# One change to a two-block transformer kernel: gated recurrence unrolled and woven, merge projections in split parts, compression by halves

## What is computed

```python
h = rmsnorm(x, g_pre_mix); z = h @ w_in
kc, vc = compress_blocks(k, pe_k, w1_k, w2_k), compress_blocks(v, ...)   # blocks of 32 tokens, stride 16: 31 of them
hid = silu(einsum('bnlgd,ldh->bngh', blocks, w1)); out = einsum('bngh,hd->bngd', hid, w2)
qk = silu(causal_conv(z[q, k], w, b))                     # 4 taps along the tokens
# gated recurrence (mLSTM), 4 heads of 128; b = cumulative sum of logf, m_t = running maximum
dw  = exp(b_t - b_s + i_s - m_t)
sqk = (q @ k.T) * dh**-0.5 * dw;   num = sqk @ v;   den = sum(sqk)
h_ml = num / max(abs(den), exp(-m_t))
h_ml = h_ml * rsqrt(mean(h_ml**2) + EPS) * g;  y_ml = sigmoid(o) * h_ml
gm = sigmoid(g_merge)                                     # three gates of width 1024
y = gm0 * (y_nsa @ w_proj_nsa) + gm1 * (y_ml @ w_proj_ml) + gm2 * (y_mem @ w_proj_mem)
x = x + rmsnorm(y @ w_out, g_post_mix)
```

## Time and profile before

| | before |
|---|---|
| median of 3 runs | 2626.87 us (2626.28 to 2628.6) |
| the profiled execution | 2629.21 us, its span 2627.4 us |
| mean granted TensorE clock of it | 0.962 |
| TensorE busy | 2470.5 us (94%) |
| VectorE, ScalarE, GpSimd busy | 662.8, 900.3, 961.7 us |
| instructions | 28732 |
| the chain that ended last | TensorE 78%, issue 10%, VectorE 4%, ScalarE 4%, GpSimd 3% |

### The profile page before, as it was taken

The page is one execution under the profiler, slowest core; times in us unless marked ns, Lnnn a source line. Parts: engine busy times, 40 slices in busy tenths (PEclk is TensorE's granted clock), DMA queues, the critical chain, the costliest instruction groups (busy, mean ns, idle before and its releaser), DMA issues.

```text
span 2627.4 us, 28732 instructions
## 1 busy us (share of the span) xinstructions
PE 2470.5 (94%) x10828; PEld 1873.9 (71%) x10828; DVE 662.8 (25%) x1319; ACT 900.3 (34%) x1552; POOL 961.7 (37%) x484
## 2 busy tenths in 40 slices
PE   6999999999889889999989999989899999999997
PEld 5888775766677678877858655477656657788776
DVE  1010312033422220113130566454511112201121
ACT  4332322154424343223221455532332223432232
POOL 3444451622352444444432321044222224344444
PEclk9999999999989999999997999899899998999999
DMA  3233234322121223223421110021113232232232
GB/s 132 96 99 96 82 95 131 109 65 68 51 74 49 80 72 96 96 77 96 140 69 40 49 41 29 1 64 48 40 57 94 83 94 65 72 97 96 79 93 92
DMA packets 74470, 204.04 MB, mean 78 GB/s; under 512 B 7184, under 2 KB 24080, under 8 KB 73872
## 3 DMA queue, kind: packets, MB, share of 16 engines
q1 hardware_dynamic: 71296, 191.92, 23.1%
q10 hardware_dynamic: 3088, 10.97, 1.2%
HBM read 199.71 MB, written 2.10 MB: 77 GB/s over the span
## 4 chain that ended last, share of the span: by engine, by line
PE 78%; issue 10%; DVE 4%; ACT 4%; POOL 3%; DMA 0%; ACTq 0%; POOLq 0%; DVEq 0%
PE bank L635 15%; PE bank L636 15%; PE bank L642 15%; PE bank L848 5%; PE bank L1068 3%; PE bank L1311 3%; POOL parts L490 2%; PE bank L785 2%; PE bank L1373 2%; PE bank L1400 1%; PE bank L1382 1%; PE bank L1288 1%; ACT parts L1603 1%; PE bank L681 1%; PE bank L1327 1%
## 5 line engine op out<-in xcount | busy, mean ns | idle before, releaser
L490 POOL TENSOR_TENSOR parts<-slot,parts 128x1024 fp32r<-128x1024 f32 (+2 forms) x344 | 762.3, 2217 | 1066.2 <-ACT parts L1603 1061.9
L635 PE MATMUL bank<-hhi,parts 128*128 128x512 f32 x1776 | 711.7, 401 | 29.6 <-POOL parts L490 18.2
L636 PE MATMUL bank<-hhi,parts 128*128 128x512 f32 x1776 | 699.8, 394 | 0.0
L1603 ACT ACTIVATE parts<-slot 128x1024 fp32r<-128x1024 f32 (+2 forms) x290 | 280.8, 970 | 842.3 <-PE bank L642 776.4
L642 PE MATMUL bank<-hlo,parts 128*128 128x512 f32 x1776 | 441.2, 390 | 0.1
L635 PEld LDWEIGHTS bank<-hhi,parts 128*128 128x128 f32 x1776 | 338.5, 191 | 124.8 <-POOL parts L490 25.2
L636 PEld LDWEIGHTS bank<-hhi,parts 128*128 128x128 f32 x1776 | 338.9, 191 | 72.7 <-issue 3.8
L642 PEld LDWEIGHTS bank<-hlo,parts 128*128 128x128 f32 x1776 | 333.4, 188 | 71.0 <-issue 1.4
L488 POOL TENSOR_TENSOR parts<-slot,lanes 128x1024 fp32r<-128x1024 f32 x54 | 103.5, 1917 | 469.6 <-PE bank L642 170.9
L2186 DVE TENSOR_TENSOR hid<-silu,bank 128x512 f32 (+1 forms) x66 | 45.4, 688 | 650.5 <-PE bank L642 630.5
L848 PE MATMUL bank<-hhi,parts 128*128 128x512 f32 x416 | 116.5, 415 | 3.0 <-POOL parts L490 3.0
(11 more groups left out here) (362 smaller groups left out, 3176.5 us busy)
## 6 DMA issues: line engine op xcount, KB each, us to landing
slot<-w SPq DMA_DIRECT2D x264, 512.0 KB, 3.5
slot<-w SPq DMA_DIRECT2D x88, 256.0 KB, 2.7
slot<-w SPq DMA_DIRECT2D x48, 448.0 KB, 3.2
hid<-w SPq DMA_DIRECT2D x8, 512.0 KB, 3.4
x<-xT ACTq DMA_DIRECT2D x1, 2048.0 KB, 10.6
hid<-headtab ACTq DMA_DIRECT2D x8, 256.0 KB, 3.9
big<-cmpw ACTq DMA_DIRECT2D x1, 2048.0 KB, 7.8
hid<-w SPq DMA_DIRECT2D x8, 256.0 KB, 2.6
```

The costliest lines, as they stand in the source:

```text
L490: pool.tensor_tensor(low, w, high.bitcast(F32), ALU.subtract).then_inc(splits, 1)
L635: pe.matmul(out, high[:, k, :], mhi[:, k, :], start=(start and k == 0), stop=False)
L636: pe.matmul(out, low[:, k, :], mhi[:, k, :], start=False, stop=False)
L1603: act.activation(parts[nth % 2][:, 0, 0:kt, :], slot[j][:, 0:kt, :], ACT.Copy).then_inc(highs, 1)
```

## The change

- Group product 0 is moved ahead of the gate product, the others one place forward; group product 3 is made with `gate_columns` between its 16th and 17th matmul. `gate_columns` also transposes the least normalisers, to columns.
- Compression alternates the two halves of the array at each of its 32 steps, instead of one half after the other.
- `SPREAD` is gone. A head's maxima are spread by one product (`spread_maxima`) while the head before runs. The least normalisers stay as columns.
- The recurrence is unrolled. The v panels of all heads are made once, in four passes with 512 moving columns (`gated_values`); the q and k panels of the next head are woven between scores and outputs of this one. The sums of the scores are made as columns (matmuls of one column, the scores stationary), as are the sums of squares. Normaliser and norm are joined: since the norm divides by the root of the mean of squares, the division by the normaliser is left out and its square enters the columns as EPS times max(den squared, least squared); one root and one reciprocal of four columns, spread once, stand for two reciprocals, an Abs and a root of 512 columns. Head 3's last two steps lie in the memory attention.
- The merge's branch projections are made from split parts, 24 or 12 fp32r matmuls each. All six panels of a turn are split by ScalarE and GpSimd, in `parts[0]`, `parts[1]` and a third buffer of 4 tiles, `quarter`. The 16 tiles of the branch outputs are split once, ahead of the loop.

The diff, cut (the functions of ScalarE and VectorE have the order of their loops here):

```diff
 
 GATES = dict(outs=1, free7=1, gates=1, acts=5, free2=1, dve=4, stats=2, free3=2, turned=1, free6=1)
-SPREAD = dict(scores=8, free4=4, free5=4)
...
+ML = dict(products=16, splits=16, highs=16, free0=6, free1=6, free4=9, free5=9, free6=1, free7=5, mspreads=4,
+          dve=48, exps=16, convs=8, scores=16, outs=4)
+ML_NORM = dict(sqs=4, stats=4, rcp=4, rinv=4, spreads=4, cats=4)
...
-        negM, emb = big8[:, 0:HEADS, :], big8[:, HEADS:2 * HEADS, :]
+        v_gated, gate_decay = big8[:, 0:TT, :], big8[:, TT:2 * TT, :]
+        quarter = tables_r[:, 0:2 * TT * P].rearrange("p (c k n) -> p c k n", c=2, k=TT)
+        merge_parts = (parts[0], parts[1], parts[0], quarter, parts[1], quarter)
+        memt = memh_r[:, :, :].rearrange("p (a b) m -> p a (b m)", b=2)
+        cat_high = [qs_r[:, 0, :], qs_r[:, 1, :], ks_r[:, 0, :], ks_r[:, 1, :], vs_r[:, :], o_r[:, 0, :], o_r[:, 1, :],
+                    var_r[:, :], *(PT_r[:, k, :] for k in range(TT)), *(memt[:, k, :] for k in range(4))]
+        cat_low = [hid_r[:, k, :] for k in range(16)]
...
+                    for p in range(16):
+                        sp.wait_ge(products, n.at("products", p + 1 - RING))
+                        dst = slot[p % RING][:, :, :]
+                        if 2 <= p < 6:
+                            first_v = panel[8] + 2
+                            src = w8[first_v:first_v + 13:4, :, 2 * (p - 2):2 * (p - 2) + 2, :].rearrange("h p k c -> p h (k c)")
+                            dst = dst.rearrange("p (h k) c -> p h (k c)", h=HEADS)
+                        else:
+                            c = p if p < 2 else p - 4
+                            src = w8[panel[8] + 4 * (c // 3) + (0, 1, 3)[c % 3]]
...
@@ -578,13 +610,19 @@
             for p in range(16):
                 split(p, p % RING, p - 1, load=1 + p // RING)
             n.past(NSA)
-            n.past(SPREAD)
-
-            split_turns(HEADS, ML, range(4), (0, 0))
+            for p in range(16):
+                split(p, p % RING, p - 1, load=1 + p // RING)
+            n.past(ML)
+            n.past(ML_NORM)
             for p in range(HEADS):
                 split(p, p, p - 1)
             n.past(MEM2)
-            split_turns(KD, MERGE, (0, 2, 4))
+            with n.turns(pool, KD, MERGE):
+                for q in range(6):
+                    kt = (8, 8, 8, 4, 8, 4)[q]
+                    high, low = (merge_parts[q][:, c, 0:kt, :] for c in range(2))
+                    pool.wait_ge(highs, n.at("highs", q + 1))
+                    pool.tensor_tensor(low, slot[q][:, 0:kt, :], high.bitcast(F32), ALU.subtract).then_inc(splits, 1)
...
+            def norm_columns_spread(i):
+
+                pe.wait_ge(rinvs, n.at("rinv", i + 1))
+                for t in range(TT):
+                    mm = pe.transpose(bank[3][:, t * P:(t + 1) * P], root_ms[:, t:t + 1].to_broadcast([P, P]), ident)
+                mm.then_inc(spreads, 1)
+
             def norm_of_tiles(events):
...
+            def gate_columns():
+
+                emptied(6, 1)
+                emptied(3, 1)
+                for t in range(TT):
+                    for r in (0, 2):
+                        mm = pe.matmul(bank[3][:, 8 * r + 4 * t:8 * r + 4 * t + 4], rows[0:4, r, t * P:(t + 1) * P],
+                                       ident[0:4, 0:4], start=True, stop=True)
+                mm.then_inc(stats, 1)
+
             pe.wait_ge(tables_loaded, 16)
             pe.wait_ge(params_loaded, 16)
             pe.wait_ge(cmp_loaded, 48)
+            group_product(0)
             pe.wait_ge(h32s, n.at("h32s"))
             emptied(7)
...
-            group_product(1)
+            group_product(2)
 
...
-            group_product(2)
-            emptied(6, 1)
-            emptied(3, 1)
-            for t in range(TT):
-                mm = pe.matmul(bank[3][:, 4 * t:4 * t + 4], rows[0:4, 0, t * P:(t + 1) * P], ident[0:4, 0:4],
-                               start=True, stop=True)
-            mm.then_inc(stats, 1)
+            emptied(1, 1)
+            h_panel(3, bank[1][:, :], between=gate_columns)
             n.past(GATES)
 
 
-            group_product(3)
             emptied(0, 2)
             emptied(1, 2)
             pe.wait_ge(dves, n.at("dve", 1))
             width = (GROUPS + 1) * CMP_N
-            for row, b, done in ((slice(0, 64), 3, stats), (slice(64, P), 6, turned)):
-                emptied(b)
-                for l in range(CMP_L):
+            emptied(3)
+            emptied(6)
+            for l in range(CMP_L):
+                for row, b, done in ((slice(0, 64), 3, stats), (slice(64, P), 6, turned)):
                     mm = pe.matmul(bank[b][:, 0:width].rearrange("p (g b) -> p g b", b=CMP_N), w1c[row, l, :],
                                    kvc[row, :, l:l + CMP_S * (CMP_N - 1) + 1:CMP_S],
                                    start=(l == 0), stop=(l == CMP_L - 1))
-                mm.then_inc(done, 1)
+                    if l == CMP_L - 1:
+                        mm.then_inc(done, 1)
             emptied(3, 1)
             pe.matmul(bank[3][:, 0:GROUPS * CMP_N], w2[:, 0:P], hidk, start=True, stop=True).then_inc(stats, 1)
             emptied(6, 1)
...
-            def normed_sum():
...
+            def gated_values(q):
+
+                high, low = (parts[(2 + q) % 2][:, part, :, :] for part in range(2))
+                pe.wait_ge(splits, n.at("splits", 2 + q + 1))
+                for m in range(24):
+                    t, j = (m // 4, m // 2 % 2) if m < 16 else ((m - 16) // 2, m % 2)
+                    if q == 0 and m < 16 and m % 4 == 0:
+                        emptied(4 + t)
+                    out = bank[4 + t][:, :].rearrange("p (h c) -> p h c", h=HEADS)
+                    mm = pe.matmul(out, (hhi if m < 16 else hlo)[:, 2 * q + j, t * P:(t + 1) * P],
+                                   (low if m < 16 and m % 2 else high)[:, j::2, :],
+                                   start=(q == 0 and m < 16 and m % 4 == 0), stop=(q == 3 and m >= 16 and j == 1))
+                mm.then_inc(products, 1)
...
+            def spread_maxima(i):
...
+                pe.matmul(bank[2][:, :], ident[0:4, i:i + 1].to_broadcast([4, P]), rows[0:4, 1, :], start=True,
+                          stop=True).then_inc(mspreads, 1)
...
+            def gated_out(i, j):
+
+                emptied(4 + j % 2, 1 + 2 * i + j // 2 + 1)
+                if j == 0:
+                    emptied(6, 1)
+                    emptied(7, 1 + i)
+                    emptied(3)
+                    pe.wait_ge(cats, n.at("cats", i))
+                for t in range(j, TT):
+                    pe.matmul(bank[3][:, t:t + 1], PT[:, j, t * P:(t + 1) * P], ones[:, 0:1], start=(j == 0 and t == 0),
+                              stop=(j == TT - 1 and t == TT - 1), skip_group_check=True)
+                mm = pe.matmul(bank[7][:, j * P:T], v_gated[:, j, i * P:(i + 1) * P], PT[:, j, j * P:T],
+                               start=(j == 0), stop=(j == TT - 1))
+                if j == TT - 1:
+                    mm.then_inc(outs, 1)
+
+            def gated_squares(i):
+
+                pe.wait_ge(sqs, n.at("sqs", i + 1))
+                for t in range(TT):
+                    mm = pe.matmul(bank[3][:, 4 + t:5 + t], var[:, t * P:(t + 1) * P], ones[:, 0:1], start=True, stop=True)
+                mm.then_inc(stats, 1)
+
+            pe.wait_ge(dves, n.at("dve"))
+            gated_panel(0, 0, 24)
+            spread_maxima(0)
+            gated_panel(1, 0, 24)
+            for q in range(4):
+                gated_values(q)
+            for i in range(HEADS):
+                o, nq, nk = 3 * i + 2, 3 * i + 3, 3 * i + 4
+                last = i == HEADS - 1
+                gated_panel(o, 0, 24)
+                gated_scores(i, 0)
+                gated_scores(i, 1)
+                if not last:
+                    gated_panel(nq, 0, 4)
+                gated_out(i, 0)
+                gated_scores(i, 2)
+                if not last:
+                    gated_panel(nq, 4, 8)
+                gated_out(i, 1)
+                gated_scores(i, 3)
+                if not last:
+                    gated_panel(nq, 8, 12)
+                gated_out(i, 2)
+                if not last:
+                    spread_maxima(i + 1)
+                    gated_panel(nq, 12, 14)
+                gated_out(i, 3)
+                if not last:
+                    gated_panel(nq, 14, 22)
+                    gated_squares(i)
+                    gated_panel(nq, 22, 24)
+                    gated_panel(nk, 0, 12)
+                    norm_columns_spread(i)
+                    gated_panel(nk, 12, 24)
+            n.past(ML)
...
-            second_query(0, 0, 24)
+            second_query(0, 0, 12)
+            gated_squares(HEADS - 1)
+            second_query(0, 12, 24)
+            norm_columns_spread(HEADS - 1)
...
-            branches_done = (n.at("cats"), n.at("free7"))
+            cat_lows = n.at("hlos")
+            n.past(CAT)
```

(89 more changed lines are left out.)

267 lines of the change are left out of this document (144 added, 123 removed).

## The result

The changed kernel takes 2579.1 us, the median of four executions (2578.2 to 2583.6), against 2627.7 us for the kernel before beside it: a ratio of 0.982, 95% interval 0.980 to 0.983. I had written 2548 us, 2530 to 2576: right that it is faster, wrong on how much, and outside the range. Run once more with the later experiments the same kernel took 2574.9 us (five executions, 2568.8 to 2581.1; ratio 0.978, 0.976 to 0.980), just inside the range. The profiled execution took 2583.6 us, its span is 2581.8. For such a one I had said 2550.3, so 33 us have to be found.

What follows compares the result with a forecast made beforehand. TensorE, busy 94% of the span, was taken as the bound. Gates -2.5, compression -14.6, recurrence -40.5, memory attention +1 and merge -22.3 sum to -78.9 from 2629.2 us profiled: 2550.3, median 2548 us, range 2530 to 2576.

Steps and rivals of the forecast that it cites:

- Merge: Merge: split fp32r matmuls replace fp32 ones, saving 2.85 us in each of 8 turns; -22.3 us in sum.
- rival (d): Merge: split parts come late, each turn gains 18.2 us and the kernel gets slower, 2694 us; chance 0.02.
- Compression: Compression: alternating halves run in pairs, 16.5 us for 33.0, against a tail longer by 1.9 us; -14.6 us.
- rival (a): Compression: the strided halves share one read, so it stays 33 us with its longer tail, 2564 us; chance 0.24.
- Value passes: Ahead of the recurrence's heads: four passes for all heads, 21.8 us, in a lead-in of 39.0 us.
- A turn's pure work: Recurrence: TensorE's work from one head's scores to the next head's, without waits, 26.6 us.
- moves ahead of the gate product, into the 6.60 us: Gates: group product 0 fills TensorE's wait for the last h tile; the stage was to change by -2.5 us.
- Does the rest keep up?: Recurrence: other engines' chain makes TensorE wait 3.2 us each head, plus 1.7 us of clock; head 31.5 us.
- copy of the k panel A+11.5, its convolution A+14.4: Recurrence: chain times in us after the q panel's end, A; the k convolution was to end at A+14.4.
- the clock: Recurrence: after each head's wait the clock halves for some 3.5 us, costing 1.7 us more per head.
- the last head: End of the recurrence: the final head's scores and outputs, with nothing woven in, take about 8 us.
- Rival (c): Recurrence: it stalls twice as much as forecast, 2562 us; chance 0.08.

Runs made afterwards that it cites:

- the five kernels whose recurrence takes 158.4 us: Five follow-up kernels, edits of the kernel after that leave the recurrence's code alone, with the same three waits of 7.45 us; their recurrence takes 158.4 to 158.5 us.
- the last kernel: Kernel after with group-0/gate banks swapped, k-panel split delayed, half q panel early, k copy earlier, compression input laid out by phase, 12 query matmuls early; 2525.6 us.
- both serial kernels: Kernel after with compression halves one after the other again, 2591.1 us; the same also reading contiguous, wrong elements, 2593.2 us in one execution.
- contiguous: Kernel after with alternating compression halves reading contiguous runs of 31 elements, not every 16th (wrong results, time only); 2567.7 us in one execution.
- exchanged banks: Kernel after with the banks of group product 0 and the gate product swapped, so group product 0 writes an empty bank; 2566.5 us.
- the last two kernels: Kernel after with bank swap, delayed split, early half q panel and earlier k copy, 2540.7 us; then also phase layout and 12 early query matmuls, 2525.6 us.

## Why the prediction was wrong, by its own steps

**Right, with their terms.** Merge: -22.0 for -22.3, with GpSimd's 100 us of work hidden beside 223 of TensorE's, so rival (d) never came near. Compression: 16.8 us for 16.5, tail within half a microsecond, rival (a) out. Memory attention +0.9 for +1. Value passes: the lead-in of the recurrence, panels and four value passes, is 39.9 us for 39.0. A turn's pure work: 25.7 for 26.6. Unrolling: nothing seen.

**Gates, +6.4.** The step "moves ahead of the gate product, into the 6.60 us" took the operands' arrival as the only condition. The bank was the other one: with it empty the stage is 5.7 us shorter. I had named what the moved product reads and not what it overwrites, and who must have emptied that.

**Recurrence, +20.1.** Three terms of "Does the rest keep up?" failed. First, "copy of the k panel A+11.5, its convolution A+14.4": it was taken at the price of a convolution alone, although the q convolution earlier in the same chain was charged for GpSimd's split. The split of the third panel of the turn starts at A+11.5 too. That is 3.6 us a turn of the 4.25 by which the wait was longer (7.45 for 3.2), shown by holding the split back; the other 0.7 is TensorE arriving sooner than I said. Over three turns 12.7 us. Second, the clock: 1.7 us for each head, measured 4.7 and 4.5 after the first and the second wait and nothing in head 0, where the same work ran without a wait before it. I had taken the 3.5 us of low clock that follow a wait of 3.30 us in the kernel before. But that is the shortest of its four cases: after waits of 3.30, 3.30, 3.30 and 3.99 us the clock there is low for 3.5, 6.8, 7.0 and 7.0 us. Over three turns +4.1 in this profile, and +0.9 in the five kernels whose recurrence takes 158.4 us: 3.2 us of this miss are that accident. Third, the last head: put at 8 us, it ran at half clock from end to end and took 12.8, +4.8 (at full clock, in the last kernel, it takes 7.1). Against these stand 2.6 us of work over-priced in three turns. The sum of turns is 33.2 + 37.9 + 37.8 + 12.8 = 121.7 for 102.5, with the lead-in's 0.9 the 20.1 us. Rival (c), "stalls twice as much", had 14 us for this mechanism and a chance of 0.08, and a head above 37 us was named as what would break the forecast; it is 37.9. The mechanism was the forecast's own and its size was off: the wait of 3.2 us that measured 7.45, the clock's 1.7 us a head and the last head's 8 us are the terms that were mis-sized.

**Untouched stages, +6.1.** In sparse attention TensorE is idle 16.7 us before (268.05 - 251.33) and 16.8 after (272.09 - 255.33), wait for wait the same; the 4.0 us are all in busy time, the same matmuls at a lower mean clock. In the kernels run here, with this stage's code unchanged, it takes 267.7 to 272.2 us, with the clock low for 20 us of it in the shortest and in the kernel before, and for 29 in the kernel after. The 2.1 us behind the merge are of the same kind (busy 432.68 for 430.42). I had put nothing for this, and the range had no room for it.

## What to carry over

When work is moved ahead into a wait, list for each of its instructions the operands, the bank or buffer that it overwrites with the instruction that empties it, and where that one stands in its engine's order. When two engines exclude each other, place every instruction of both on one time line for the whole turn; pricing one meeting and not the next put 3.6 us into each of three turns here. And a wait of TensorE costs more than its length: fill it, with later useful matmuls if there are any, for a wait of 7.4 us here took a further 1.9 to 4.7 us of clock.

## What the runs showed of the hardware that I had not expected

- While only one half of the array's rows worked at a time, the granted clock stayed at its lower level, with TensorE busy all the time: for 32 to 33 us in both serial kernels, where it had fallen just before, and for 31 in the kernel before, where it fell 1.6 us into the stage. With the halves alternating it came back within 5 us (kernel after, and contiguous), or never fell (exchanged banks, and the last two kernels).
- The price of a wait in clock is not a function of its length: after 3.8 to 4.1 us of standing still the lower level lasted 3.5 us in one turn and 10.25 in the next, in two kernels alike; after 7.45 us, 13.7, 13.7 and 20.5 us in the kernel after, and 6.8 to 7.0, 13.5 and 20.5 in five others.
- 26 matmuls without use in a wait of 7.4 us made the turns 4.5 us shorter than in the kernel after, 1.7 and 4.6 shorter than in the five others.
- The same stage with the same code and the same waits differs by up to 4.5 us between kernels, with where the half clock falls. The part ahead of the gates, which no edit touches, ends between 1331.6 us (one half after the other) and 1340.4 us (one after the other and contiguous). Part of a difference between two profiles belongs to that, and a few microseconds in a stage that no edit touches are no sign of a mechanism.
